# The last layer norm of a two-layer decoder trunk: scale ahead of time, mean and shift summed by TensorE

## The reference, cut to what matters

```
def layer_norm(x, g, b):
    mu = jnp.mean(xf, axis=-1, keepdims=True)
    var = jnp.mean(xc * xc, axis=-1, keepdims=True)      # xc = xf - mu
    return xc * lax.rsqrt(var + LN_EPS) * g + b
...
        y = conv_ffn(x, ffn_w_up[i], ffn_conv_w[i], ffn_conv_b[i], ffn_w_down[i])
        x = layer_norm(ALPHA * x + y, ln_g[i, 1], ln_b[i, 1])
    return x
```

## Time and profile before

| | |
|---|---|
| median of 3 runs | 2240.12 us (2238.68 to 2240.33) |
| profiled execution, its own time | 2239.88 us |
| its span, first to last instruction | 2238.2 us |
| granted TensorE clock, mean | 0.993 |
| TensorE busy | 2197.7 us (98%) |
| TensorE weight loads | 2030.4 us (91%) |
| VectorE busy | 1343.0 us (60%) |
| ScalarE busy | 1039.0 us (46%) |
| GpSimd busy | 212.6 us (9%) |
| read from and written to memory | 405.46 MB, 2.18 MB |

### The profile page before, as it was taken

One profiled execution on the slowest core, in us unless ns is written; L12 is line 12 of the kernel. 1 busy time (PEld: TensorE's weight loads), 2 busy tenths in 40 slices (PEclk: granted clock), 3 DMA queues, 4 the chain that ended last, 5 costly groups with the idle time before them and its releaser, 6 DMA issues.

```text
span 2238.2 us, 40969 instructions
## 1 busy us (share of the span) xinstructions
PE 2197.7 (98%) x15259; PEld 2030.4 (91%) x15259; DVE 1343.0 (60%) x1805; ACT 1039.0 (46%) x1380; POOL 212.6 (9%) x206
## 2 busy tenths in 40 slices
PE   9999999999999999999999999999999999999996
PEld 7998799999999988888899998889999999988885
DVE  5565686665666554447655565576666566654445
ACT  4554355454545443335444444355545454543332
POOL 2000050000000000003420120041000000000001
PEclk9999999999999999999999999999999999999998
DMA  8444566666666655555755654656666666665553
GB/s 262 152 152 154 180 185 190 187 187 187 188 187 187 188 187 188 188 187 157 215 174 153 199 159 141 195 163 208 187 188 187 187 187 187 187 225 188 187 187 105
DMA packets 206951, 408.70 MB, mean 183 GB/s; under 512 B 12652, under 2 KB 13756, under 8 KB 206620
## 3 DMA queue, kind: packets, MB, share of 16 engines
q1 hardware_dynamic: 200192, 385.92, 56.4%
q0 software_dynamic: 5776, 21.34, 3.4%
q10 hardware_dynamic: 908, 0.43, 0.1%
HBM read 405.46 MB, written 2.18 MB: 182 GB/s over the span
## 4 chain that ended last, share of the span: by engine, by line
PE 96%; DVE 3%; ACT 0%; issue 0%; DMA 0%; DVEq 0%; ACTq 0%
PE ps L1163 19%; PE ps L1165 18%; PE ps L1166 18%; PE ps L1149 12%; PE ps L1150 12%; PE ps L1151 12%; PE ps L1271 1%; PE ps L1278 1%; PE ps L1289 1%; PE ps L1290 1%; PE ps L1270 1%; DVE res L938 1%; PE ps L1288 0%; PE ps L1222 0%; DVE cg L795 0%
## 5 line engine op out<-in xcount | busy, mean ns | idle before, releaser
L744 DVE TENSOR_TENSOR w_lo<-raw,w_hi 128x1024 fp32r<-128x1024 f32 x728 | 913.6, 1261 | 667.9 <-ACT w_hi L468 666.8
L468 ACT ACTIVATE w_hi<-raw 128x1024 fp32r<-128x1024 f32 x728 | 771.4, 1060 | 984.9 <-PE ps L1166 543.6
L1163 PE MATMUL ps<-xh,w_lo 128*128 128x256 f32 x3584 | 1011.6, 282 | 13.0 <-DVE xl L782 8.7
L1166 PE MATMUL ps<-xh,w_hi 128*128 128x256 f32 x3584 | 1001.1, 279 | 0.0
L1165 PE MATMUL ps<-xl,w_hi 128*128 128x256 f32 x3584 | 1001.0, 279 | 0.0
L1163 PEld LDWEIGHTS ps<-xh,w_lo 128*128 128x128 f32 x3584 | 675.1, 188 | 16.7 <-DVE xl L782 9.7
L1165 PEld LDWEIGHTS ps<-xl,w_hi 128*128 128x128 f32 x3584 | 675.2, 188 | 0.4
L1166 PEld LDWEIGHTS ps<-xh,w_hi 128*128 128x128 f32 x3584 | 674.7, 188 | 0.0
L1149 PE MATMUL ps<-w_lo,hid_h 128*128 128x512 f32 x704 | 278.4, 396 | 0.0
L1151 PE MATMUL ps<-w_hi,hid_h 128*128 128x512 f32 x704 | 278.4, 396 | 0.0
L1150 PE MATMUL ps<-w_hi,hid_l 128*128 128x512 f32 x704 | 278.4, 395 | 0.0
(11 more groups left out here) (156 smaller groups left out, 1501.9 us busy)
## 6 DMA issues: line engine op xcount, KB each, us to landing
raw<-in_ffn_w_up_dram SPq DMA_DIRECT2D x352, 512.0 KB, 3.6
raw<-in_ffn_w_down_dram SPq DMA_DIRECT2D x176, 512.0 KB, 4.6
raw<-in_b_w_qkvf_dram SPq DMA_DIRECT2D x96, 512.0 KB, 4.1
raw<-in_a_w_qkv_dram SPq DMA_DIRECT2D x40, 512.0 KB, 4.4
raw<-in_a_w_o_dram SPq DMA_DIRECT2D x32, 512.0 KB, 4.7
raw<-in_b_w_o_dram SPq DMA_DIRECT2D x32, 512.0 KB, 4.3
bias<-rel_by_distance POOLq DMA_DIRECT2D x4, 1024.0 KB, 6.6
bias<-minus_cumulated_decay POOLq DMA_DIRECT2D x4, 1024.0 KB, 6.2
```

Of the source, the lines that this page charges most:

```text
L468: act.activation(w_hi[:, loc % RING], raw[:, loc % RING], ACT.Copy).then_inc(high_ready, 1)
L744: dve.tensor_tensor(w_lo[:, s], raw[:, s], w_hi[:, s].bitcast(FP32), ALU.subtract).then_inc(low_ready, 1)
L1163: pe.matmul(o, w_lo[:, slot, k % 2, cols], xh[:, k, :], start=(k == 0 and j % 2 == 0), stop=False, skip_group_check=True)
L1166: last = pe.matmul(o, w_hi[:, slot, k % 2, cols], xh[:, k, :], start=False, stop=(k == KT - 1), skip_group_check=True)
```

## The change

The scale g is multiplied into `res` group by group (`gains`): for groups 0 to 2 during the down projection, four chunks after the group's statistics were taken; for group 3 behind the norm. The output is then x*g*rstd + (nmr*g + b). The bracket is summed by TensorE into PSUM, by two matmuls per piece of one token tile and 512 columns: the weights are `coefT`, in which row 0 holds the high part of nmr for each token, row 32 the low part, and row 96 ones; the moving operand holds g in rows 0 and 32 and b in row 96, as a high part `rows_hi` and a low part `rows_lo`. VectorE writes nmr into columns of `coef`, TensorE turns it, ScalarE copies it to `coefT`. VectorE then makes each of the eight pieces with one `scalar_tensor_tensor` that reads PSUM (four banks in turn). SP stores the pieces of token tile 0, ScalarE's queue those of tile 1, eight transfers of 256 KB. GpSimd and ScalarE no longer take part in the arithmetic on `res`; GpSimd clears and loads `coef`, `rows` and `gain`. The new tiles lie where `xh` and `xl` lay.

```
@@ sync
+            for i in range(OUT_GROUPS):
+                cols = slice(i * COLS, (i + 1) * COLS)
+                sp.wait_ge(fin_ready, 2 * i + 1)
+                sp.dma_start(ov[:, 0, cols], res[:, 0, cols]).then_inc(out_done, 16)
+            sp.wait_ge(out_done, 16 * MT * OUT_GROUPS)
@@ gpsimd
-            for i, src in enumerate((ln_g, ln_b)):
-                gp.dma_start(lnfull[:, i, :], src[1, 1:2, :].to_broadcast([P, D])).then_inc(full_in, 16)
-            gp.wait_ge(full_in, 32)
-            for m in range(MT):
-                gp.wait_ge(z0_ready, 3 * KC + m + 1)
-                own.link(gp.tensor_tensor(res[:, m, GP_COLS], res[:, m, GP_COLS], lnfull[:, 0, GP_COLS], ALU.mult))
-                gp.tensor_tensor(res[:, m, GP_COLS], res[:, m, GP_COLS], lnfull[:, 1, GP_COLS], ALU.add).then_inc(fin_gp, 1)
+            gp.dma_start(gain[:, :], ln_g[1, 1:2, :].to_broadcast([P, D])).then_inc(full_in, 16)
+            gp.memset(coef[:, :, :], 0.0)
+            own.link(gp.memset(rows[:, :], 0.0))
+            for row, src in ((0, ln_g), (32, ln_g), (96, ln_b)):
+                gp.dma_start(rows[row:row + 1, :], src[1, 1:2, :]).then_inc(rows_in, 16)
+            gp.memset(coef[:, :, 96:97], 1.0).then_inc(coef_ready, 1)
@@ scalar, last down projection
-                split_run(b4, KC + AHEAD, OUT_GROUPS * FC - KC - (AHEAD if l == DEPTH - 1 else 0))
+                split_run(b4, KC + AHEAD, FC - KC)
+                act.wait_ge(rows_in, 48)
+                for i in range(2):
+                    cols = slice(i * D // 2, (i + 1) * D // 2)
+                    act.activation(rows_hi[:, cols], rows[:, cols], ACT.Copy).then_inc(rows_high, 1)
+                    split_run(b4, (i + 1) * FC + AHEAD, FC)
+                split_run(b4, 3 * FC + AHEAD, FC - AHEAD)
@@ scalar, end
-            act.wait_ge(norm_ready, 4)
-            for m in range(MT):
-                act.activation(res[:, m, GP_COLS], res[:, m, GP_COLS], ACT.Identity, scale=rstd[:, 2, m:m + 1],
-                               bias=nmr[:, m:m + 1]).then_inc(z0_ready, 1)
+            act.wait_ge(coef_turned, 1)
+            act.activation(coefT[:, :], ps[:, X_BANK, 0:SEQ], ACT.Copy).then_inc(coefT_ready, 1)
+            for i in range(OUT_GROUPS):
+                cols = slice(i * COLS, (i + 1) * COLS)
+                act.wait_ge(fin_ready, 2 * i + 2)
+                act.dma_start(ov[:, 1, cols], res[:, 1, cols]).then_inc(out_done, 16)
@@ vector, last down projection
+            def gains(n):
+                dve.wait_ge(full_in, 16)
+                cols = slice(n * COLS, (n + 1) * COLS)
+                for m in range(MT):
+                    last = dve.tensor_tensor(res[:, m, cols], res[:, m, cols], gain[:, cols], ALU.mult)
+                return last
...
+                    split_run(b4, n * FC + LOW_AHEAD, 4)
+                    gains(n - 1)
+                    split_run(b4, n * FC + LOW_AHEAD + 4, 4)
+                    if n <= 2:
+                        cols = slice((n - 1) * D // 2, n * D // 2)
+                        dve.wait_ge(rows_high, n)
+                        dve.tensor_tensor(rows_lo[:, cols], rows[:, cols], rows_hi[:, cols].bitcast(FP32), ALU.subtract).then_inc(rows_low, 1)
+                    split_run(b4, n * FC + LOW_AHEAD + 8, FC - 8 - (LOW_AHEAD if n == OUT_GROUPS - 1 else 0))
@@ vector, end
+            own.link(dve.tensor_copy(nmr_hi[:, :], nmr[:, :]))
+            dve.tensor_copy(coef[:, :, 0], nmr_hi[:, :].bitcast(FP32))
+            own.link(dve.tensor_tensor(nmr_lo[:, :], nmr[:, :], nmr_hi[:, :].bitcast(FP32), ALU.subtract))
+            dve.wait_ge(coef_ready, 1)
+            dve.tensor_copy(coef[:, :, 32], nmr_lo[:, :].bitcast(FP32)).then_inc(coef_ready, 1)
+            own.link(gains(OUT_GROUPS - 1))
+            for i in range(OUT_GROUPS):
+                cols = slice(i * COLS, (i + 1) * COLS)
                 for m in range(MT):
+                    t = MT * i + m
+                    dve.wait_ge(shift_ready, t + 1)
+                    dve.scalar_tensor_tensor(res[:, m, cols], res[:, m, cols], rstd[:, 2, m:m + 1], ps[:, shift_bank(t), :],
                                              ALU.mult, ALU.add).then_inc(fin_ready, 1)
@@ tensor, end
+            pe.wait_ge(rows_low, 2)
+            pe.wait_ge(coef_ready, 2)
+            for m in range(MT):
+                last = pe.transpose(ps[:, X_BANK, m * P:(m + 1) * P], coef[:, m, :], ident[:, :])
+            last.then_inc(coef_turned, 1)
+            pe.wait_ge(coefT_ready, 1)
+            for t in range(MT * OUT_GROUPS):
+                i, m = t // MT, t % MT
+                if t >= 4:
+                    pe.wait_ge(fin_ready, t - 3)
+                o = ps[:, shift_bank(t), :]
+                mine, cols = coefT[:, m * P:(m + 1) * P], slice(i * COLS, (i + 1) * COLS)
+                pe.matmul(o, mine, rows_lo[:, cols], start=True, stop=False)
+                pe.matmul(o, mine, rows_hi[:, cols], start=False, stop=True).then_inc(shift_ready, 1)
```

More of the change, by code:

```diff
@@ L50 @@
 LN_EPS = 1e-5
-GP_COLS = slice(D - 5 * P, D)
 DVE_FULL = (0, 1, 2, 4, 6)
@@ L153, in trunk @@
         nmr = sb("nmr", [P, MT])
+        nmr_hi = sb("nmr_hi", [P, MT], F32R)
+        nmr_lo = sb("nmr_lo", [P, MT], F32R)
+        coef = sb("coef", [P, MT, P])
+        coefT = sb("coefT", [P, SEQ], F32R)
         warm = sb("warm", [P, 1])
@@ L157, in trunk @@
         with ExitStack() as later:
-            lnfull = sb("lnfull", [P, 2, D], FP32, later)
+            gain = sb("gain", [P, D], FP32, later)
+            rows = sb("rows", [P, D], FP32, later)
         xh_hold = sb("xh_hold", [P, KT * SEQ])
-        xl = sb("xl", [P, KT, SEQ], F32R)
+        with ExitStack() as first:
+            xl = sb("xl", [P, KT, SEQ], F32R, first)
+        with ExitStack() as later:
+            rows_hi = sb("rows_hi", [P, D], F32R, later)
+            rows_lo = sb("rows_lo", [P, D], F32R, later)
+        xl_hold = sb("xl_hold", [P, KT * SEQ])
         with ExitStack() as mix:
@@ L255, in trunk @@
         fin_ready = sem("fin_ready")
-        fin_gp = sem("fin_gp")
+        coef_ready = sem("coef_ready")
+        coef_turned = sem("coef_turned")
+        coefT_ready = sem("coefT_ready")
+        shift_ready = sem("shift_ready")
+        rows_in = sem("rows_in")
+        rows_high = sem("rows_high")
+        rows_low = sem("rows_low")
         full_in = sem("full_in")
@@ L274, in backwards, with shift_bank @@
             return src.rearrange("p (b t) -> p b t", t=P)[:, :, ::-1]
+        def shift_bank(t):
+            return X_BANK + (t + 1) % 4
         def wait_free(eng, s, turns):
@@ L725, in _ @@
             layer_norm(4)
[L726 to L729 removed]
+            act.wait_ge(coef_turned, 1)
+            act.activation(coefT[:, :], ps[:, X_BANK, 0:SEQ], ACT.Copy).then_inc(coefT_ready, 1)
+            ov = out[0].rearrange("(m p) d -> p m d", p=P)
+            for i in range(OUT_GROUPS):
+                cols = slice(i * COLS, (i + 1) * COLS)
+                act.wait_ge(fin_ready, 2 * i + 2)
+                act.dma_start(ov[:, 1, cols], res[:, 1, cols]).then_inc(out_done, 16)
         @block.vector
@@ L1106, in mlp @@
                     residual((n - 1) % 2, (t0, t1)[(n - 1) % 2] + (n - 1) // 2, CH_DOWN[l] + n * FC, n - 1, pieces)
-                    split_run(b4, n * FC + LOW_AHEAD, FC - (LOW_AHEAD if l == DEPTH - 1 and n == OUT_GROUPS - 1 else 0))
+                    if l < DEPTH - 1:
+                        split_run(b4, n * FC + LOW_AHEAD, FC)
+                        continue
+                    split_run(b4, n * FC + LOW_AHEAD, 4)
[6 more added lines that the diff above has]
+                    split_run(b4, n * FC + LOW_AHEAD + 8, FC - 8 - (LOW_AHEAD if n == OUT_GROUPS - 1 else 0))
                 n = OUT_GROUPS
@@ L1126, in _ @@
             layer_norm(4, last)
-            dve.wait_ge(full_in, 32)
-            for i in range(3):
-                cols = slice(i * COLS, min((i + 1) * COLS, GP_COLS.start))
-                for m in range(MT):
[L1132 to L1136, removed]
+            own.link(dve.tensor_copy(nmr_hi[:, :], nmr[:, :]))
[6 more added lines that the diff above has]
+                cols = slice(i * COLS, (i + 1) * COLS)
+                for m in range(MT):
+                    t = MT * i + m
+                    dve.wait_ge(shift_ready, t + 1)
+                    dve.scalar_tensor_tensor(res[:, m, cols], res[:, m, cols], rstd[:, 2, m:m + 1], ps[:, shift_bank(t), :],
                                              ALU.mult, ALU.add).then_inc(fin_ready, 1)
```

3 lines of the change are left out of this document (added).

## The result

| | before | after |
|---|---|---|
| median | 2239.77 us (2238.68 to 2240.33, 4 runs) | 2272.38 us (2271.21 to 2273.26, 4 runs) |
| span of the profiled execution | 2238.2 us | 2270.3 us |
| start of the step that follows the shift | 2221.54 | 2258.15 |
| from there to the end of the span | 16.7 us | 12.15 us |

The time is 1.0143 of the time before, interval 1.0131 to 1.0155: 32.6 us slower, where 4.7 us less was forecast. The third and fourth lines split it: the tail behind the shift, where all the forecast's working lay, became 4.5 us shorter, and the stretch ahead of it became 36.6 us longer.

The account below looks back on a forecast made before the run. The end was taken as bound by store bytes ready late, behind VectorE's tail. Rebuilding the tail moves the span from 2238.2 to 2233.5 us, minus 4.7, giving 2235.2 us; range 2233.8 to 2237.2.

Parts of the forecast that it names:

- the first sentence of the reading: Whole kernel: TensorE is busy nearly throughout, so edits outside its stream count only where it has nothing to do.
- beside the path: Down projection: VectorE's added multiplies and differences and ScalarE's copies fit into idles, costing nothing; uncovered 6.5 and 2.1 us.
- the slower one, TensorE starved at the boundaries: Rival, group boundaries: VectorE's added work stops TensorE and the clock falls; plus 7.9 us, 2247.8; chance 4%.
- Four small steps until TensorE's turn: Tail from 2221.54: four VectorE instructions on 128x2 at 0.19 us each, done at 2222.30.
- The turn: Tail: TensorE turns two 128x128 blocks at half clock, about 0.8 us with the wake, until 2223.15.
- At half clock: Tail: first matmul pair ready after 1.19 us, each further piece 0.855 us, so TensorE sets the pace at first.
- The first add: Tail: VectorE's first add, reading PSUM, starts at 2224.90, once piece 0 is ready at 2224.85.
- The clock rises: Tail: full clock returns after 3.4 to 5.6 us of TensorE work; middle taken, 2228.1.
- the last add: Tail: VectorE's add of piece 7 starts at 2230.25 and ends at 2230.95.
- Behind the last add: End of tail: last store takes issue 0.02, first byte 0.9, bytes 0.70, end 0.95, sum 2.57 us, to 2233.5.
- VectorE disturbed by GpSimd: Old tail: GpSimd's work on its 640 columns stretches VectorE's instructions, 4.9 us; the change removes these instructions.
- The two small multiplies for group 3: Tail: VectorE multiplies group 3 by the gain, 0.69 us each, hidden under turn, copy and first pair; uncovered 1.35 us.

Follow-up runs that it names:

- the small tiles last: Kernel after with its four small tiles (nmr_hi, nmr_lo, coef, coefT) allocated behind hid_l instead of ahead of xh: 2236.03 us, 0.9981 of before.
- the kernel before with the pad of 160 bytes: Kernel before with 160 unused bytes ahead of xh, none of the change's work: 2194.16 us, 0.9824 of before.

## Why the prediction was wrong

**What failed.** The step is the first sentence of the reading: TensorE is busy nearly throughout, "so an edit outside its stream counts only where TensorE has nothing to do". It holds for edits that leave TensorE's operands where they are, and the change moved them. The forecast costed the instructions beside the path and found them free; it has no term for the new tiles, of which it says nothing, and so put their place at nothing without a reason. That term is plus 36.6 us at the shift. A 1% change of TensorE's pace is 22 us here, almost five times the whole gain at stake in the tail, so the bound that the first rows show, TensorE busy without a gap, should have led to the question what could change its pace, not only what could stop it. None of the rivals asked it; the slower one, TensorE starved at the boundaries, was slower for another reason and did not occur.

**The tail, term by term.** From the first small step to the end: 12.0 us forecast, 12.15 measured after and 12.1 with the small tiles last.
- Four small steps until TensorE's turn: 0.78 us (2258.15 to 2258.93), forecast 0.76 without the wake. Right.
- The turn 0.41 and not 0.8, since the clock was still 1.00: it fell between 2259.5 and 2260.0, 5.0 us after the last product ended (2254.82, the idle of 4.11 ahead of the turn). The row of before that the forecast used, a fall about 2 us after the last product, was one execution's; the last section has others. With the copy, 0.38 as in the earlier trace rows, the first matmul starts 1.67 after the shift; forecast 2.1.
- At half clock the matmuls come 0.42 to 0.43 apart, as in the earlier trace rows, and 0.23 later. The first add starts 3.00 after the shift, forecast 3.36.
- The clock rises 3.4 us after TensorE goes on, earlier than the 4.45 taken and at the lower end of the range of 3.4 to 5.6. With both, the last add ends 8.74 us after the first small step, forecast 9.41.
- Behind the last add 3.4 us pass and not 2.57. The stores are the term that was too small: with two queues the bytes don't flow evenly (320, 225 and 283 GB/s in the three half microseconds from 2266.0, 365 just ahead of them, 393 and 402 behind). So 0.67 us came in early and 0.8 went out late: the sum is right by two errors that cancel.
- VectorE disturbed by GpSimd, 4.9 us: gone, as forecast. The two small multiplies for group 3 take 1.29 and hide under turn and copy.
- Beside the path: TensorE 62.00 of 62 at the third boundary, and no idle at all between two matmuls of the last down projection (2007.3 to 2254.8). Costs nothing, as forecast.

Of the weight that the forecast gave to a rule of the pages: the Trainium skill (DMA: Bandwidth & Descriptors, Bandwidth) asks for transfers of 1 MiB or more; here stores of 256 and of 512 KB end the kernel within 0.4 us of each other, so the rule sets nothing in this tail, as the forecast chose.

**What stays open.** Shown is that the distance between the tiles of the two operands, by its remainder by 256 bytes, changes TensorE's pace, and that moving both together does not bring the loss. That it is the distance to `w_hi` and `w_lo`, and not to another tile ahead of `xh`, is concluded from the pace being the same whether VectorE and ScalarE work or not. Not shown is by what mechanism, nor why one distance can have two paces. Nearest at hand is that a matmul's reads of its moving operand and the reads of the weight load beside it meet in the same part of memory, more or less often with the distance; no run here separates the two. The Trainium skill (SBUF — State Buffer, SBUF: two separate sides) says that on the engines' side only the port pair shared by VectorE and GpSimd causes contention and that TensorE waits on no other engine. The traces agree: 349.7 and 349.9 ns with VectorE idle and busy. The Trainium skill also says (TensorE: Matmul & The Clock Gate, Step-by-step: what each phase is for) that TensorE reads through two independent ports, so that loading the next weights takes no bandwidth from the running matmul. Taken alone, that gives no reason for the pace to hang on the distance, and it does, by 340 to 360 ns a triple; whether the two reads are what disturbs each other, no run shows. Remainder 224 was not tried, nor the distances for the two kinds of product set apart from each other: the best of both, 340.0 and 226.7 ns, would be another 2112 x 2.2 ns = 4.6 us, an estimate.

## What to carry to other kernels

When one engine is busy without a gap, ask of every edit whether it moves a buffer that this engine reads, and allocate new small tiles behind the large ones. Count its instructions in equal windows of both kernels before looking anywhere else: the same work at the same granted clock, with no wait and fewer instructions per window, is a change of pace. And a pad of a few tens of bytes between the operands of a product is worth a sweep over 256 bytes, with several executions of each, since one distance can have two paces: here it gave over ten times what the redesigned tail gave.

## What the runs showed of the hardware

- Distance of the two operands by 256 bytes, at full clock, three matmuls of 256 columns each with its own weight load: 340 ns at 192 (353 in one short run of each trace), 350 at 32 (353 in one projection), 353 at 64 (340 in one short run), 352 or 356 at 160, 356 at 128, 360 at 96 and 0. Where two are given, the pace changed only behind a break in the stream. For 512 columns: 226.7 at 0, 228.9 at 192, 232.4 at 128, 233.3 at 32, 64 and 160, 234.3 at 96.
- So a matmul of 256 columns costs 113.3 to 120.0 ns in a stream.
- The pace hardly depends on VectorE: 349.7 ns where it is idle and 349.9 where it is busy in the kernel before, 360.0 and 360.2 in the kernel after.
- The clock falls at quite different times after the last product. In the kernel before it was 2.0 us (2218.2 to 2220.2), in the kernel after 5.0, with the turn of 0.41 shortly ahead of it, and in the kernel before with the pad of 160 bytes, whose tail is the same code, 5.1. The last product there ends at 2173.0, and its windows show:

```profile
2173.00:2173.50 0.50, 0.01 (x1) 0.00 (x0) 0.50 (x2) 0.00 (x0) 0.00 (x0) 1.00 0.00 0
2178.00:2178.50 0.50, 0.00 (x0) 0.00 (x0) 0.50 (x1) 0.09 (x1) 0.50 (x1) 0.65 0.00 0
```

- So a fall of the clock read off one execution is no term for a forecast to half a microsecond. The rise came 3.4 us after TensorE had gone on.
- Stores of 256 KB on two queues land in 2.7 and 3.0 us; the rate dips to 225 GB/s in the half microsecond from 2266.5 and is 393 and 402 GB/s behind the dip. With the stores merged on one queue it is 353 to 399 GB/s while the bytes of a store flow.
